# Place sums in float32r, constant matmuls in the pauses of routing, slot rows between the halves of gate/up 0

## The reference, cut to what matters

```python
g_val, g_idx = lax.top_k(softmax(t @ w_group + b_group), 1)          # best group
chosen = e_logits of that group                                       # t @ w_expert + b_expert
e_val, e_idx = lax.top_k(softmax(chosen), 2)                          # two experts in it
combine = one_hot(g_idx) * g_val * (one_hot(e_idx) * e_val / sum(e_val))
for each expert e:  y += (silu(t @ w_gate[e]) * (t @ w_up[e]) * combine[:, e]) @ w_down[e]
```

## Time and profile before

| what | value |
|---|---|
| runs of the kernel before, us | 916.2, 916.29, 920.12 |
| profiled execution, us | 921.16 |
| its span, first to last instruction, us | 919.4 |
| TensorE matmul busy | 791.4 us, 86% |
| VectorE busy | 390.9 us, 43% |
| ScalarE busy | 225.7 us, 25% |
| GpSimd busy | 193.3 us, 21% |
| mean granted TensorE clock | 0.919 |

### The profile page before, as it was taken

One profiled execution on the slowest core, in us unless ns is written; L12 is line 12 of the kernel. 1 busy time (PEld: TensorE's weight loads), 2 busy tenths in 40 slices (PEclk: granted clock), 3 DMA queues, 4 the chain that ended last, 5 costly groups with the idle time before them and its releaser, 6 DMA issues.

```text
span 919.4 us, 10352 instructions
## 1 busy us (share of the span) xinstructions
PE 791.4 (86%) x3995; PEld 435.7 (47%) x3995; DVE 390.9 (43%) x686; ACT 225.7 (25%) x382; POOL 193.3 (21%) x198
## 2 busy tenths in 40 slices
PE   1777879799999999988399969996999999898787
PEld 1656735534433333346388745445433333343355
DVE  6996542532232322154465568516233223222344
ACT  3332215301111101043344444422211101101142
POOL 6873402121110110000460264002211111010000
PEclk7688979699999999998799979996999999999979
DMA  6043063969999999981945670174399999999711
GB/s 207 1 120 118 13 267 131 417 272 422 422 421 420 421 420 421 414 308 60 283 122 183 232 217 9 63 306 180 125 421 420 421 420 421 421 421 421 282 56 46
DMA packets 58402, 247.03 MB, mean 269 GB/s; under 512 B 16594, under 2 KB 17648, under 8 KB 33392
## 3 DMA queue, kind: packets, MB, share of 16 engines
q1 hardware_dynamic: 53632, 240.35, 65.1%
q0 software_dynamic: 1600, 4.26, 2.4%
q10 hardware_dynamic: 3120, 1.74, 0.9%
HBM read 244.72 MB, written 1.60 MB: 268 GB/s over the span
## 4 chain that ended last, share of the span: by engine, by line
PE 74%; issue 10%; DVE 8%; ACT 3%; POOL 2%; DMA 1%; ACTq 0%; SPq 0%; POOLq 0%; DVEq 0%
PE PS L1734 23%; PE PS L1510 11%; PE PS L1765 11%; PE PS L1775 5%; PE PS L1934 3%; PE PS L1667 3%; PE PS L1705 2%; PE PS L1609 2%; PE PS L1543 2%; PE PS L1914 2%; PE PS L1893 2%; PE PS L1624 1%; POOL qrs L687 1%; PE PS L1746 1%; PE PS L1903 1%
## 5 line engine op out<-in xcount | busy, mean ns | idle before, releaser
L1734 PE MATMUL PS<-ring,xe 128*64 128x512 f32 x1024 | 232.7, 608 | 15.9 <-issue 13.6
L1734 PEld LDWEIGHTS PS<-ring,xe 128*64 128x64 f32 x1024 | 80.4, 140 | 164.9 <-issue 164.9
L1765 PE MATMUL PS<-ring,actT 128*64 128x512 f32 x512 | 116.9, 599 | 1.7 <-DVE actT L1285 1.4
L614 POOL COPY xe<-xg 128x512 f32 x60 | 47.0, 784 | 300.5 <-PE PS L1734 298.1
L1299 DVE TENSOR_TENSOR olo<-PS,ohi 128x512 fp32r<-128x512 f32 x64 | 44.3, 692 | 123.5 <-ACT ohi L852 123.5
L1285 DVE COPY actT<-PS 128x256 f32<-128x256 f32 x32 | 13.6, 424 | 177.3 <-PE PS L1746 177.3
L992 DVE TENSOR_TENSOR ringr<-ring,dwh 128x1024 fp32r<-128x1024 f32 x40 | 52.4, 1324 | 56.9 <-ACT dwh L725 56.9
L1510 PE MATMUL PS<-ringr,hTh 128*128 128x512 f32 x160 | 65.2, 407 | 12.6 <-DVE hTl L983 6.4
L852 ACT ACTIVATE ohi<-PS 128x512 fp32r<-128x512 f32 x64 | 38.2, 597 | 153.0 <-PE PS L1765 153.0
L844 ACT ACTIVATE act<-PS 128x256 f32<-128x256 f32 x32 | 12.3, 384 | 227.3 <-PE PS L1734 227.3
L1765 PEld LDWEIGHTS PS<-ring,actT 128*64 128x64 f32 x512 | 34.7, 137 | 67.0 <-issue 67.0
(11 more groups left out here) (321 smaller groups left out, 1065.4 us busy)
## 6 DMA issues: line engine op xcount, KB each, us to landing
ring<-in_moe_w_gate SPq DMA_DIRECT2D x64, 1024.0 KB
ring<-in_moe_w_up SPq DMA_DIRECT2D x64, 1024.0 KB
ring<-in_moe_w_down SPq DMA_DIRECT2D x64, 1024.0 KB, 24.4
ring<-in_nat_w_qkv SPq DMA_DIRECT2D x6, 2048.0 KB
ring<-in_ple_w_gate SPq DMA_DIRECT2D x4, 2048.0 KB
ring<-in_s_w_out SPq DMA_DIRECT2D x2, 2048.0 KB
ring<-in_nat_w_o SPq DMA_DIRECT2D x2, 2048.0 KB
ring<-in_s_w_in SPq DMA_DIRECT2D x1, 2048.0 KB
```

What stands on the lines that cost most here:

```text
L614: pool.tensor_copy(xe[:, e % 4, :, :], xg[:, :, bass.ds(first, CAP)]).then_inc(S("xe_ready"), 1)
L1734: ins = mm(PS[CAP * h_:CAP * h_ + CAP, 0, :].rearrange("p (u f) -> p u f", u=2), xe[:, (2 * p + h_) % 4, k, :], wv[h_][:, k], start=k == 0 ...
L1765: ins = mm(PS[CAP * h_:CAP * h_ + CAP, 2 + n, :], actT[:, k, CAP * h_:CAP * h_ + CAP], wd[h_][:, k, 512 * n:512 * n + 512], start=k == 0, ...
```

## The change

Four things change, in both layers:

- `msk` and `below` become two planes of one float32r tile `mb`, and `ones` and `tri` become float32r tiles (read as float32 by `spread_rows` and by the zeroing of banks 6 and 7). `places` sums both halves of the tokens in one matmul each: `below` of half 0 and of half 1 are read twice (64 columns), `msk` of half 0 is added to the second half (32 columns), and `tri` by `msk` (64 columns) closes. Then two matmuls of 64 columns make the tally.
- A new function `constant(n)` issues n float32r matmuls of `ones` by `ones`, 128 x 128 by 512 columns, into bank 6, each starting afresh. Nothing reads the result.
- `constant(2)` stands behind the second half's transposes, `constant(14)` behind the second router, `constant(5)` behind the places.
- `spread_rows` moves from behind the gather to between the two `gate_up` calls of pair 0.

```diff
-        tri = new("tri", [P, P])
+        tri = new("tri", [P, P], F32R)
-        ones = new("ones", [P, P])
+        ones = new("ones", [P, P], F32R)
...
-        msk = at("msk", [P, TT, NE], F32, RX + 2432)
-        below = at("below", [P, TT, NE], F32, RX + 2688)
+        mb = at("mb", [P, TT, 2, NE], F32R, RX + 2432)
+        msk, below = mb[:, :, 0], mb[:, :, 1]
...
             def places(i):
 
                 pe.wait_ge(S("msk_ready"), i + 1)
+                dst = PS[:, 4, 0:TT * NE].rearrange("p (t e) -> p t e", t=TT)
                 for t in range(TT):
-                    dst = PS[:, 4, NE * t:NE * t + NE]
-                    mm(dst, ones[:, :], below[:, 0], start=True, stop=False)
-                    mm(dst, ones[:, :], below[:, 1], start=False, stop=False)
-                    if t:
-                        mm(dst, ones[:, :], msk[:, 0], start=False, stop=False)
-                    ins = mm(dst, tri[:, :], msk[:, t], start=False, stop=True)
-                ins.then_inc(S("pos_done"), 1)
-                for w, of in enumerate((msk, below)):
-                    for t in range(TT):
-                        ins = mm(PS[:, 5, 64 + NE * w:64 + NE * w + NE], ones[:, :], of[:, t], start=t == 0, stop=t == 1)
+                    mm(dst, ones[:, :], bc(mb[:, t, 1], 1, TT), start=t == 0, stop=False)
+                mm(dst[:, 1], ones[:, :], mb[:, 0, 0], start=False, stop=False)
+                mm(dst, tri[:, :], msk, start=False, stop=True).then_inc(S("pos_done"), 1)
+                for t in range(TT):
+                    ins = mm(PS[:, 5, 64:64 + 2 * NE], ones[:, :], mb[:, t].rearrange("p w e -> p (w e)"),
+                             start=t == 0, stop=t == 1)
                 ins.then_inc(S("tally_done"), 1)
+
+            def constant(n):
+
+                for _ in range(n):
+                    mm(PS[:, 6, :].rearrange("p (b n) -> p b n", b=4), ones[:, :], bc(ones[:, :], 1, 4),
+                       start=True, stop=True)
...
             def moe(i):
                 router(i, 0)
                 x_T(i, 1)
+                constant(2)
                 router(i, 1)
+                constant(14)
                 places(i)
+                constant(5)
...
                 for k in range(KD):
                     gather(i, k)
-                spread_rows(i)
                 for p in range(NP):
                     gate_up(i, p, 0, 4)
+                    if p == 0:
+                        spread_rows(i)
                     gate_up(i, p, 4, KD)
```

More of the change, by code:

```diff
@@ L537, in _ @@
             pool.memset(mask[:, :], 1.0)
-            pool.memset(tri[:, :], 1.0)
-            pool.memset(ones[:, :], 1.0)
+            pool.memset(tri[:, :].bitcast(F32), 1.0)
+            pool.memset(ones[:, :].bitcast(F32), 1.0)
             link(pool.memset(negh[:, :], 0.0))
@@ L1207, in route @@
                         ALU.is_gt))
-                tt(msk[:, :, :], eq[:, :, 0], eq[:, :, 1], ALU.add)
-                tt(below[:, :, :], low[:, :, 0], low[:, :, 1], ALU.add).then_inc(S("msk_ready"), 1)
+                tt(msk, eq[:, :, 0], eq[:, :, 1], ALU.add)
+                tt(below, low[:, :, 0], low[:, :, 1], ALU.add).then_inc(S("msk_ready"), 1)
                 ts(ngm[:, :], gmx[:, :, 0], -1.0, None, ALU.mult)
@@ L1616, in _ @@
             for k in range(2):
-                mm(PS[:, 6 + k, :].rearrange("p (b n) -> p b n", b=4), zrow[:, :], bc(ones[0:1, :], 1, 4),
+                mm(PS[:, 6 + k, :].rearrange("p (b n) -> p b n", b=4), zrow[:, :], bc(ones[0:1, :].bitcast(F32), 1, 4),
                    start=True, stop=False)
@@ L1713, in spread_rows @@
                     pe.wait_ge(S("diag_ready"), 2 * TT * i + TT * n + TT)
-                    mm(PS[:, 2 + n, :], ones[:, :], diag[:, n].rearrange("p j t s -> p (j t s)"), start=True, stop=True)\
+                    mm(PS[:, 2 + n, :], ones[:, :].bitcast(F32), diag[:, n].rearrange("p j t s -> p (j t s)"), start=True, stop=True)\
                         .then_inc(S("row_done"), 1)
```

## The result

| | before | after |
|---|---|---|
| median of 20 runs each on one chip, us | 919.94 (913.7 to 924.47) | 915.32 (910.57 to 918.9) |
| ratio, 95% interval | | 0.9948 [0.9931, 0.9965] |
| profiled execution, us | 921.16 | 913.65 |
| its span, us | 919.4 | 911.9 |

The change makes the kernel faster by 0.52%, with 0.35 to 0.69% as the interval: 4.8 us, 3.2 to 6.3. That lies on the bound of 0.5% that the prediction named.

The account below looks back on a forecast made before the run. Alternating TensorE and VectorE waits in each layer's routing stretch, which delay the weight stream, were taken as the bound; 2.3 + 0.4 = 2.7 us a layer, 5.4 in all, gave 916.29 - 5.4 = 910.9 us, range 905.5 to 915.0.

Parts of the forecast that it names:

- The level: Whole kernel: starting time taken as the median of the runs, 916.29 us, below the profiled execution's 921.16.
- The place sums: Before `pos_done`: four float32r matmuls replace 14 float32 instructions, saving 2.3 us a layer, between 1.3 and 2.6.
- steps like a float32 entry: Place sums: if small float32r matmuls step like float32 entries, four take 1.08 us at 0.50 clock.
- The other estimate for the low clock: Place sums: by the documented weight-load time, four matmuls take 0.3 us less at half clock, the sum 6.0 us.
- The gather: Gather in both layers: the clock often falls behind the constants but rises somewhat earlier, saving 0.4 us a layer.
- The slot rows: Two float32 matmuls moved between the halves of gate/up 0: 1.72 us, order changes no sum, so nothing gained or lost.
- The constants' cost: Three groups in TensorE's pauses before router, places and gather: nothing; at worst 1.1 and 0.2 us before the places.
- VectorE in between: Layer 0: faster router lets the `gf` CAST between the `hlo` subtractions, 1.4 us more saved, 909.5 us; chance 0.08.
- an earlier router waits for the same `hlo`: Routing stretch: speeding up router 1 gains nothing, since VectorE's `gf` CAST ends with GpSimd's `hlo` subtractions.
- The clock holds: Places and gather: clock stays at 1.00 through the pauses, saving 10.6 us, 905.7 us; chance 0.2.
- Only the small sums: Clock stays down, places save 2.1, constants cost 1.1 and 0.2, gather unchanged: 2.9 us saved, 913.4; chance 0.22.
- Slower: Constants cost what float32 costs, 0.86 us each, and outlast the pauses: about 928 us; chance 0.05.

Follow-up runs that it names:

- e1: Kernel before with only the place sums in float32r, no constants, slot rows behind the gather; ratio 0.9958, median 915.34 us.
- e5: Changed kernel with 26 constants instead of 14 ahead of the places and 12 instead of 5 ahead of the gather; ratio 0.9881, median 910.03 us.
- e3: Changed kernel without any constant matmul; ratio 0.9962, median 916.07 us.
- e8: Changed kernel with slot rows behind the gather, `hlo` in pieces outside the route, and 2, 16 and 12 constants; ratio 0.9852, median 906.42 us.
- e9: Changed kernel with 26 constants instead of 14 ahead of the places, still five ahead of the gather; ratio 0.9922, median 911.98 us.
- e10: Changed kernel with 12 constants instead of 5 ahead of the gather, still fourteen ahead of the places; ratio 0.9954, median 917.23 us.
- e2: Changed kernel with the slot rows moved back behind the gather; ratio 0.995, median 914.66 us.

## Why the prediction was wrong, point by point

**The level: this step failed.** "I carry the difference over: 916.29 - 5.4 = 910.9" took the median of three runs for the kernel's level. Those three are the first of the 20 runs in the table, and two of them are among its six lowest; the median of the 20 is 919.94, and the three medians beside the experiments are 920.15, 921.4 and 920.3. The level was 3.65 us too low. By its own sum the prediction would have given 919.94 - 5.4 = 914.5, and its other figure, 915.8 "for one like" the profiled execution, is 0.5 us from the result; that is in part luck, since the profiled execution happened to lie only 1.2 us above the median of the 20. The range was built from the costs of the mechanisms alone and held nothing for the level, though the profiled time stood 4.9 us above the median used. On the right level the same range would have ended at 918.7. The errors of the mechanisms, below, do not put the time outside it.

**The place sums: right.** 2.3 us a layer was forecast, between 1.3 and 2.6; they gave 2.34 and 2.56. This is nearly the whole effect (e1). The case that "steps like a float32 entry", 1.08 us at 0.50, was borne out by e1 with 1.10. The other estimate for the low clock, 0.3 us less, was not: the matmuls begin 0.21 us apart or more at 0.50, and 0.11 to 0.13 only at 1.00 (e5).

**The gather: right in kind, too large.** It said that the clock would fall again behind the constants and that both gathers would begin low: so they do, in every kernel with 14 and 5 constants. The 0.4 us a layer for an earlier rise does not show: 9.62 us with constants, 9.59 without. What the constants do help is the places, by 0.49 to 0.86 us in both layers; the prediction had put 0.2 us a layer of that into its 2.3.

**The slot rows: mis-sized.** "The order changes no sum: nothing" was argued from TensorE having no pause. It has none, but the matmuls themselves take longer in that order: 0.38 us a layer, 0.76 in all, which eats what the constants bring. The trace of after shows where: within either kind one step follows the other after 0.42 to 0.43 us, as before, and steps of 0.47 to 0.53 stand at or next to the changes between gate/up and slot rows (from 181.3 to 184.2 us). The old order changes between full-width and gate/up matmuls once, the new one three times. What TensorE does there was not taken apart. That nothing would be late for pair 1 was right: the chain goes from gate/up 0 through `act` to pair 1 as before.

**The constants' cost: right.** No group outlasts its pause.

With the terms so corrected the sum is 4.90 for the places, 0.16 and 0.04 for the small columns, less 0.76: 4.3 us, and 919.94 - 4.3 = 915.6 stands 0.3 from the median. The forecast of 5.4 lies inside the interval of the change, 3.2 to 6.3, although the gather was put 0.8 too high and the slot rows 0.76 too low in cost: the interval is too wide to tell.

**The rivals.** *VectorE in between*: its condition came true, the router of layer 0 ran at 1.00 (as it did in e3, without constants) and the CAST got in. Its price did not: it expected the next wait at `eid`, 1.6 us on, and the very next operation, `pen`, waited for the second `hlo`. So "an earlier router waits for the same `hlo`" was wrong for the CAST and right for the places. The 1.55 us won at the router come back as 1.43 between CAST and places. The Trainium skill (GPSIMD Engine Reference, 1. Specifications) says that GpSimd shares its SBUF interfaces with VectorE and names two cases of contention, VectorE's two-port modes and two SBUF inputs. `pen` has two, and the trace agrees with 2.37 us beside `hlo` and 0.24 away from it (e8). Which of the two the CAST would be, with its one input, no run here shows. *The clock holds*: it did not, with pauses of 3.03 and 0.55 us left in layer 0, 2.63 and 1.24 in layer 1; with both filled (e5) the gathers gain 10.22 + 9.96 - 7.54 - 7.50 = 5.14 us, close to the 5.44 that this rival priced. *Only the small sums* is nearest in mechanism, since the gathers gained nothing that shows; but the clock was not down ahead of the places, the cost of 1.3 that it put on the constants did not come, and its 913.4 too hangs on the level. *Slower*: the constants cost 0.25 us each in the pauses (3.46/14), far from the 0.51 from which it decides.

## What to carry to other kernels

A predicted time is a level plus a change: where few runs are shown and the profiled one lies away from their median, the level belongs into the range like any other term. A long GpSimd instruction beside a chain of short VectorE operations can hold some of them up though they share no data; look for short operations that end with it, and move it or cut it. Matmuls that are to keep the clock up gave the stretch its gain here when they filled both pauses up to the next work on the path (e5, e8). With one pause left, the gather or the constants themselves ran at 0.50 in the executions profiled (e9, e10).

## What the runs showed of the hardware

- Some of VectorE's small operations stand still while a GpSimd elementwise instruction runs: beside `hlo`, the CAST takes up to 2.30 us and `pen` 2.37 (after), where alone they take 0.18 and 0.24 (e8). Others do not: beside the same `hlo`, `lg`, MAX8 and FIND_INDEX8 take 0.26, 0.17 and 0.16 us (after, 158.94 to 159.67 us), as they do alone (e8).
- The granted clock fell to 0.50 after pauses of 3.03 and 2.63 us (after: at 165.4, 0.3 us into the places, and at 629.6 in layer 1, 1.3 us after the places began) and around one of 1.8 us (e9: at 167.5 in layer 0, within the pause, and at 635.1 in layer 1, when the gather had been running for 0.8 us). With pauses of 0.33 and 0.23 us it stayed at 1.00 (e5).
- Float32r matmuls of 32 and 64 columns begin 0.11 to 0.13 us apart at 1.00 (e5) and 0.21 to 0.24 at 0.50 (e1), though they have a sixteenth to an eighth of the columns of those that take 0.21 and 0.43.
- Two float32 matmuls of 512 columns and the gate/up matmuls of a pair take 0.38 us longer together when the two stand between the halves of the gate/up (1.91 + 7.23, after) than when they stand ahead of it (1.72 + 7.04, before and e2).
